# The last block's delta rule: first inverses between z's weight steps, solve two items earlier, new load order, z's Silu from a tanh

## Chip, cores, metric

One core of one Trainium2 chip. The metric is the device time of one execution of the whole program in microseconds (us); the kernel before has a median of 2697.6 us over three runs.

## The reference, cut to what matters

The program is a small network over 512 tokens of width 1024 (batch 1): two layers with attention and 16 experts, and then one last block, to which the change belongs. All is fp32.

```python
def second_block(x, ...):
    h = rmsnorm(x, ln1)
    qkv_a, z_a, b_a, a_a, q_b, k_b, v_b = split(h @ w_in)
    y_a = gated_deltanet(qkv_a, z_a, b_a, a_a, ...)      # 4 heads of 128
    y_b = dilated_attention(heads(q_b), heads(k_b), heads(v_b), slopes)   # 8 heads of 64
    x = x + concat([y_a, y_b]) @ w_out
    h = rmsnorm(x, ln2)
    x = x + (silu(causal_dwconv(h @ w_gate)) * (h @ w_up)) @ w_down
    return rmsnorm(x, ln_f)
# in gated_deltanet, by chunks: a = strict(k_beta k^T * decay); (1 + a) sol = [v*beta, k_beta*exp(g)];
# then a scan over the chunks: v_new = u - w S; o = q_dec S + a_qk v_new; S = S*dl + k_dec^T v_new
# y_a = o * rsqrt(mean(o*o)) * norm_gain * silu(z)
```

The kernel takes chunks of 128 tokens, so there are four (t = 0 to 3), and four heads (h).

## The kernel before, in words

The engines run five hand-written programs. Each walks the same list of pieces and does its own part of each, in the order of the list; semaphores tie them together, and every engine takes its work strictly in its own order. For the stretch of this change the list is `second_plan()` (L492 to L549), and `between()` in each engine's program walks it.

**Weights.** Weights come as loads of up to 1 MB into slots (`weight_steps()`, L97). Slots 0 to 2 are the ring RING; slot 3 is the tail of X (X[:, 4:6]). SP issues them in order and waits until the slot is free. For a product in two parts (high and low, fp32r), ACT copies a step of 1024 columns to WHL as its high part (L1474), and DVE (L2015) or POOL (L2793), by turns, subtracts to get the low part. PE then makes three matmuls where one would do. The copies run two steps ahead of PE; they do not cross into the output weights' steps before the piece `early`. WHL shares its memory with the attention's buffers (EB2, ET2, SB2, YH, YBT: "WIDE" in the profile), so the first three steps of the output weights also wait for the last low part of the attention's output ("behind", `V["y2", 7]`). The output weights are `loads[third]` on. Before, the turn through the slots went on from the input weights, so the first of them falls on slot 3, whose memory is the delta rule's scratch WS; SP waits there for the end of the solve (`P["du", 6, 3]`, L793).

**Part one of the list (k = 0 to 15).** PE makes q and k of the attention (`col`), then vb and z (`tok`, four steps each, four token tiles per step; z's four tiles end in the last step). Beside them the delta rule is prepared: norms of q and k (`square`, `sum`, `unit`), turned keys and values, scalars, `decay` h (matmul gb; DVE's differences L2609, ACT's exponentials into WS[h] (the decay) and CMS[h]), and products on POOL (`values`, `keys`, `kdec`). The piece `zsilu` stands at the end: ACT has copied z out of PE's banks (L1838) and then puts Silu over it in place (L1871), which takes a table load before and one behind.

**Part two (items k = 0 to 36).** `attend` k is a pipeline over the 32 pairs of attention head and query tile: score matmul (PE L1255), bias, maximum and sign (DVE L2559 to L2564), exponential (ACT L1809, one item later), transposes (L848) and their copy (L1817), values (PE L1269), scaling (DVE L2575); a pair of heads is turned at the end of its last item (`ybT`, copy L1823). Between the parts of the attention stand those of the delta rule:

- `head` h (k = 0 to 3): PE makes kk (L1326), bb (L1323) and kq (L1326 again). DVE (L2618 to L2630): AT = kk * WS, AT = bb * AT, U0 = mask of AT, then identity minus it, a copy DL, AQ = kq * WS behind POOL's causal mask of WS[h] (L2909), and q times its decay.
- `first` h: transposes of U0 and ACT's copy (L1875). `mask` n, h: POOL's product of AT with the mask of level n (L2917).
- the solve by doubling, levels n = 1 to 6, four heads each: `cm` (PE L1342, ACT's copy L1881), then `onward` (PE L1349 du and L1354 dt, DVE L2635 and L2639).
- `nw` h (L1362, L1885), then the scan: `vnew` t (PE L1374, L1376; ACT L1891), `out` t (PE L1386 ds, L1392/L1393 o; ACT's square L1897; DVE's state L2652/L2655, sum L2659, mean L2661), `gate` t (ACT's root L1902; DVE L2667 to L2676, the last of them with z), `flip` t (transposes L848, copy L1906).

Behind the items comes the tail: `y2` j (high and low parts of the mixed output, L1915 and L2680), `early` (the copies of the output weights' first three steps), and `mix` n, t (output projection of tile t, L1237 to L1239).

**Banks.** PE's eight banks are two rings here: `flow` (0 to 3) for `col`, `tok`, `attend` and `mix`, and `rule` (4 to 7) for the delta rule. Taking a bank waits for the named release of the piece that had it four takes before, for instance `(V, ("kkd", h))`: DVE's first product of head h.

What fixes the place of the pieces before:

```python
for k in range(37):
    if k < 36: plan.append(("attend", k))
    if k < 4: plan.append(("head", k))
    if 1 <= k <= 4: plan += [("first", k - 1), ("mask", 1, k - 1)]
    if 0 <= k - 5 < 24: plan.append(("onward", *wy[k - 5]))
```

## Time and profile before

| | |
|---|---|
| runs | 2700.8, 2697.6, 2692.08 us (median 2697.6) |
| the profiled execution | 2695.96 us, its span 2693.8 us |
| granted clock of TensorE over the span | 0.972 of 2.4 GHz |
| PE busy | 93% of the span |
| DVE, ACT, POOL busy | 48%, 37%, 15% |
| the stretch of `second_plan`'s items to the last turned tile | about 2078 to 2268 us |

The times are those of the slowest (here the only) core. Busy shares are means over stages that differ; the stretches below show the stage in question. The granted clock is 1.00 at 2.4 GHz and 0.50 at 1.2 GHz; a value between is a mean over both. A bracket behind a row says how long the engine had been idle before it, and which instruction ended that.

### The profile page before, as it was taken

What the parts mean: (1) busy time and instruction counts of PE and PEld (TensorE: products, weight loads), DVE (VectorE), ACT (ScalarE), POOL (GpSimd) and SP (SyncE); (2) the same over time, 40 slices, a digit from 0 to 9 for tenths busy, and PEclk for the clock granted to TensorE, in tenths of its full rate; (3) what the DMA queues carried; (4) which work ended last, traced back from release to release, by engine and by line L of the source; (5) the groups of instructions that cost most, each with busy time, mean ns of one, the idle gap of its engine ahead of it and who ended that gap; (6) DMA issues with size and microseconds to landing.
All of it is one profiled execution on the core that took longest, in us unless ns stands there. A gap on an engine that the chain in (4) does not pass through costs nothing.

```text
span 2693.8 us, 35458 instructions
## 1 busy us (share of the span) xinstructions
PE 2513.7 (93%) x13952; PEld 1531.4 (57%) x13952; DVE 1294.7 (48%) x2483; ACT 991.1 (37%) x1862; POOL 408.5 (15%) x276
## 2 busy tenths in 40 slices
PE   6998997899999997997969999998999898999998
PEld 4875565433333332775744344442767787788886
DVE  3596435344444444586352333334664655442342
ACT  5216542334444443526433222223344333322222
POOL 0222102001111101223100000001114311122221
PEclk8999999899999999998989999999999899999999
DMA  6216744699999996320139999998120002222221
GB/s 262 81 47 233 272 153 185 248 335 377 386 386 389 389 389 239 117 78 1 49 147 422 421 421 421 421 421 328 56 86 20 13 22 105 86 94 94 94 87 55
DMA packets 85467, 567.71 MB, mean 211 GB/s; under 512 B 11760, under 2 KB 12016, under 8 KB 20280
## 3 DMA queue, kind: packets, MB, share of 16 engines
q1 hardware_dynamic: 79944, 550.15, 52.0%
q0 software_dynamic: 3616, 11.80, 2.0%
q10 hardware_dynamic: 1744, 3.51, 0.4%
q8 instruction: 112, 1.84, 0.3%
q14 instruction: 51, 0.42, 0.0%
HBM read 550.74 MB, written 14.68 MB: 210 GB/s over the span
## 4 chain that ended last, share of the span: by engine, by line
PE 47%; DVE 3%; DMA 1%; ACT 1%; issue 1%; DVEq 0%; ACTq 0%
PE PS L1108 12%; PE PS L1225 4%; PE PS L1223 4%; PE PS L1224 4%; PE PS L1237 3%; PE PS L1239 3%; PE PS L1238 3%; PE PS L1182 2%; PE PS L1213 2%; PE PS L848 1%; DMA RF<-in_w_down_dram 1%; PE PS L1349 1%; PE PS L1354 1%; PE PS L1269 1%; PE PS L1255 1%
## 5 line engine op out<-in xcount | busy, mean ns | idle before, releaser
L2793 POOL TENSOR_TENSOR WHL<-RING,WHL 128x1024 fp32r<-128x1024 f32 x64 | 172.8, 2700 | 1324.9 <-ACT WHL L1474 1324.9
L1474 ACT ACTIVATE WHL<-RING 128x1024 fp32r<-128x1024 f32 x129 | 134.6, 1047 | 200.4 <-PE PS L1239 129.3
L1223 PE MATMUL PS<-RR,WHL 128*128 128x512 f32 x512 | 205.0, 400 | 2.0 <-DVE RR L2546 1.1
L1225 PE MATMUL PS<-RR,WHL 128*128 128x512 f32 x512 | 203.2, 397 | 0.0
L1224 PE MATMUL PS<-RR,WHL 128*128 128x512 f32 x512 | 201.5, 394 | 0.0
L1108 PE MATMUL PS<-RING,RF 128*64 128x512 f32 x816 | 184.9, 596 | 0.7 <-issue 0.7
L1108 PE MATMUL PS<-WIDE,RF 128*64 128x512 f32 x792 | 183.0, 599 | 0.0
L2015 DVE TENSOR_TENSOR WHL<-RING,WHL 128x1024 fp32r<-128x1024 f32 x65 | 81.8, 1260 | 165.7 <-ACT WHL L1474 159.5
L1760 ACT ACTIVATE RF<-PS,MODS,MSC 128x128 f32<-128x128 f32 x192 | 73.2, 445 | 182.8 <-PE PS L1182 130.5
L1108 PE MATMUL PS<-RF 128*64 128x512 f32 x544 | 127.5, 596 | 0.5 <-DMA RF<-in_w_down_dram 0.5
L1108 PE MATMUL PS<-X,RF 128*64 128x512 f32 x528 | 123.0, 597 | 0.6 <-DMA X<-in_w_down_dram 0.6
L1108 PEld LDWEIGHTS PS<-RING,RF 128*64 128x64 f32 x816 | 55.8, 137 | 111.7 <-issue 104.9
L1108 PEld LDWEIGHTS PS<-WIDE,RF 128*64 128x64 f32 x792 | 54.1, 137 | 113.7 <-issue 109.2
L1239 PE MATMUL PS<-WHL,AS 128*128 128x512 f32 x288 | 114.2, 397 | 0.0
L2475 DVE TENSOR_TENSOR RF<-PS,RF 64x512 f32<-64x512 f32 x64 | 43.5, 680 | 142.0 <-ACT RF L1741 142.0
L2099 DVE SCALAR_TENSOR_TENSOR AR<-AR,VEC 128x497 f32<-128x497 f32 (+29 forms) x180 | 111.7, 697 | 0.0
L1223 PEld LDWEIGHTS PS<-RR,WHL 128*128 128x128 f32 x512 | 96.1, 188 | 27.1 <-issue 4.2
L1224 PEld LDWEIGHTS PS<-RR,WHL 128*128 128x128 f32 x512 | 96.1, 188 | 25.3 <-issue 1.7
L1225 PEld LDWEIGHTS PS<-RR,WHL 128*128 128x128 f32 x512 | 96.1, 188 | 23.2
L2448 DVE TENSOR_TENSOR RF<-PS,RF 64x512 f32<-64x512 f32 x64 | 43.6, 681 | 117.9 <-ACT RF L1706 115.5
L1237 PE MATMUL PS<-WHL,AS 128*128 128x512 f32 x248 | 98.5, 397 | 0.8 <-DVE RF L2310 0.8
L1238 PE MATMUL PS<-WHL,AS 128*128 128x512 f32 x248 | 98.3, 396 | 0.0
(404 smaller groups left out, 5151.0 us busy)
## 6 DMA issues: line engine op xcount, KB each, us to landing
RING<-in_w_gate_dram SPq DMA_DIRECT2D x60, 1024.0 KB, 16.0
WIDE<-in_w_down_dram SPq DMA_DIRECT2D x52, 1024.0 KB, 11.6
RING<-in_ada_w_dram SPq DMA_DIRECT2D x48, 1024.0 KB, 6.1
RING<-in_w_up_dram SPq DMA_DIRECT2D x44, 1024.0 KB, 7.5
X<-in_w_gate_dram SPq DMA_DIRECT2D x39, 1024.0 KB
AR<-in_w_up_dram SPq DMA_DIRECT2D x37, 1024.0 KB, 9.8
RF<-in_w_down_dram SPq DMA_DIRECT2D x31, 1024.0 KB, 13.7
RING<-in_w_in_dram SPq DMA_DIRECT2D x30, 1024.0 KB, 5.1
```

The source lines that it names most:

```text
L1108: ins = e.matmul(a[r:r + 64, :], xs[:, j, 0:64], w[:, i, :], start=begin and i < 2, stop=end and i > 1)
L1223: e.matmul(o, h[:, j, :], HTH2[:, j, :], start=j == 0, stop=False)
L1224: e.matmul(o, h[:, j, :], HTL2[:, j, :], start=False, stop=False)
L1225: ins = e.matmul(o, lo[:, j, :], HTH2[:, j, :], start=False, stop=j == 7)
L1237: e.matmul(o, hi(j)[:, z], h[:, i, :], start=j == 0, stop=False)
L1238: e.matmul(o, hi(j)[:, z], lo[:, i, :], start=False, stop=False)
L1239: ins = e.matmul(o, lo_(j)[:, z], h[:, i, :], start=False, stop=j == k - 1)
L1474: e.activation(h, load_buffer(ld)[:, js, cs], ACT.Copy).then_inc(act, A(("hi", st["i"])))
L1760: e.activation(xs[:, :, a0:a0 + w_], o[:, b0:b0 + 2 * w_].rearrange("p (e s) -> p e s", e=2), ACT.Identity, bias=MODS2[:, l, 24 + jj, s:s ...
L2015: e.tensor_tensor(lo, load_buffer(loads[st["load"]])[:, js, cs], h.bitcast(F32), ALU.subtract).then_inc(dve, V(("lo", st["i"])))
L2099: e.scalar_tensor_tensor(y, UB[:, i, t0 + lo + d:t0 + hi + d], VEC[:, w:w + 1], y, ALU.mult, ALU.add).then_inc(dve, V(*([("conv", l, s)] i ...
L2793: e.tensor_tensor(lo, load_buffer(loads[st["load"]])[:, js, cs], h.bitcast(F32), ALU.subtract).then_inc(pool, G(("lo", st["i"])))
```

## The change

In the list: `causal` h (POOL's mask of the decay) becomes a piece of its own behind `decay`; the old `head` is split in three. `last` h is the copy DL. `head` h keeps kk, bb and U0 and goes to k = 13, 14, 15 and behind them (heads 0 to 3), so two of them stand between z's steps and two behind the last. `query` h is kq, AQ and q's decay and stays at items 0 to 3, with `first` h and `mask` 1, h now in the same item. `cm`, `onward`, `nw` and the scan's first pieces go two items earlier; `vnew` 3 and all before it lie in the items now, and `gate` 2 leads the tail.

z: ACT takes tanh(z/2) out of the bank in place of the copy; DVE makes (tanh + 1) * z, with z read from the bank, at `zsilu`; the bank is free after that. The missing 0.5 goes into the last product of `gate`.

Loads: the turn through the slots starts anew at the output weights, so they take slots 0, 1, 2 and then 3.

```diff
--- before.py
+++ after.py
@@ -181,7 +181,8 @@
     for ld in loads:
-        turn, slots = (0 if ld["slots"] != slots and slots[:3] != ld["slots"][:3] else turn + 1), ld["slots"]
+        new = ld["slots"] != slots and slots[:3] != ld["slots"][:3]
+        turn, slots = (0 if new or ld is loads[third] else turn + 1), ld["slots"]
         k = slots[turn % len(slots)]
@@ -513,38 +514,39 @@
             plan += [("decay", k - 10), ("keys", k - 10)]
+        if 11 <= k <= 14:
+            plan.append(("causal", k - 11))
+        if k == 13:
+            plan += [("last", h) for h in range(4)] + [("head", 0)]
         if k == 14:
...
         if k >= 14:
-            plan += [("kdec", 2 * (k - 14)), ("kdec", 2 * (k - 14) + 1)]
-    plan.append(("zsilu",))
+            plan += [("kdec", 2 * (k - 14)), ("kdec", 2 * (k - 14) + 1), ("head", k - 13)]
+    plan += [("head", 3), ("zsilu",)]
 
...
               ("out", 2), ("flip", 1), ("vnew", 3), ("gate", 2), ("out", 3), ("flip", 2), ("gate", 3), ("flip", 3)]
-    starts = {("vnew", 0): 30, ("out", 0): 31, ("vnew", 1): 32, ("gate", 0): 32, ("out", 1): 33, ("flip", 0): 34}
+    starts = {("vnew", 0): 28, ("out", 0): 29, ("vnew", 1): 30, ("gate", 0): 30, ("out", 1): 31, ("flip", 0): 32,
+              ("vnew", 2): 33, ("gate", 1): 34, ("out", 2): 35, ("flip", 1): 36, ("vnew", 3): 36}
     for k in range(37):
...
         if k < 4:
-            plan.append(("head", k))
-        if 1 <= k <= 4:
-            plan += [("first", k - 1), ("mask", 1, k - 1)]
-        if 0 <= k - 5 < 24:
-            plan.append(("onward", *wy[k - 5]))
-        if 0 <= k - 4 < 24:
-            n, h = wy[k - 4]
+            plan += [("query", k), ("first", k), ("mask", 1, k)]
+        if 0 <= k - 3 < 24:
+            plan.append(("onward", *wy[k - 3]))
+        if 0 <= k - 2 < 24:
+            n, h = wy[k - 2]
             plan.append(("cm", n, h))
...
                 plan.append(("mask", n + 1, h))
-        if 26 <= k < 30:
-            plan.append(("nw", k - 26))
-        while chunks and k >= starts.get(chunks[0], 35 if chunks[0][0] != "flip" else 36):
+        if 24 <= k < 28:
+            plan.append(("nw", k - 24))
+        while chunks and k >= starts.get(chunks[0], 37):
             plan.append(chunks.pop(0))
-            if chunks and chunks[0] not in starts:
-                break
-    assert chunks[0] == ("out", 2)
-    plan += [("out", 2), ("flip", 1), ("y2", 4), ("y2", 5), ("y2", 6), ("y2", 7), ("vnew", 3), ("gate", 2), ("early",),
+    assert chunks[0] == ("gate", 2)
+    plan += [("gate", 2), ("y2", 4), ("y2", 5), ("y2", 6), ("y2", 7), ("early",),
              ("out", 3), ("flip", 2), ("mix", 0, 0), ("gate", 3), ("mix", 0, 1), ("mix", 0, 2), ("flip", 3), ("mix", 0, 3)]
@@ -1290,7 +1292,7 @@
                     elif what == "tok":
-                        tokens(flow, (k[0],), A, 8, k[1], lambda j: HTH2[:, j, :], lambda j: HTL2[:, j, :])
+                        tokens(flow, (k[0],), V if k[0] == "z" else A, 8, k[1], lambda j: HTH2[:, j, :], lambda j: HTL2[:, j, :])
                     elif what == "attend":
@@ -1317,14 +1319,18 @@
                         h, = k
-                        for name, f, free in (("kk", 4 + h, "kkd"), ("bb", 0, "at"), ("kq", h, "aq")):
-                            o = bank(rule, (name, h), (V, (free, h)))
-                            if name == "bb":
-                                ins = e.matmul(o, HSEL[:, 128 * h:128 * h + 128], BR, start=True, stop=True)
-                            else:
-                                for z in tiles4:
-                                    ins = e.matmul(o[:, z], C[:, 4 + h, z], C[:, f, z], start=True, stop=True)
-                            ins.then_inc(pe, P((name, h)))
+                        o = bank(rule, ("kk", h), (V, ("kkd", h)))
+                        for z in tiles4:
+                            ins = e.matmul(o[:, z], C[:, 4 + h, z], C[:, 4 + h, z], start=True, stop=True)
+                        ins.then_inc(pe, P(("kk", h)))
+                        o = bank(rule, ("bb", h), (V, ("at", h)))
+                        e.matmul(o, HSEL[:, 128 * h:128 * h + 128], BR, start=True, stop=True).then_inc(pe, P(("bb", h)))
+                    elif what == "query":
+                        h, = k
+                        o = bank(rule, ("kq", h), (V, ("aq", h)))
+                        for z in tiles4:
+                            ins = e.matmul(o[:, z], C[:, 4 + h, z], C[:, h, z], start=True, stop=True)
+                        ins.then_inc(pe, P(("kq", h)))
                     elif what == "first":
@@ -1832,11 +1838,12 @@
                         weights()
-                        if n == 6:
-                            for t in range(4):
-                                e.wait_ge(pe, P[name, t])
-                                e.activation((VB if name == "vb" else Z)[:, t, :], held(name, t), ACT.Copy
-                                             ).then_inc(act, A((name, t)))
+                        for t in range(4 if n == 6 else 0):
+                            e.wait_ge(pe, P[name, t])
+                            if name == "vb":
+                                e.activation(VB[:, t, :], held(name, t), ACT.Copy).then_inc(act, A((name, t)))
+                            else:
+                                e.activation(Z[:, t, :], held(name, t), ACT.Tanh, scale=0.5).then_inc(act, A(("ztanh", t)))
                     elif what == "attend":
@@ -1865,10 +1872,6 @@
                         e.activation(KDC, KDC, ACT.Exp).then_inc(act, A(("kdc",)))
-                    elif what == "zsilu":
-                        e.wait_ge(act, A["z", 3])
-                        for t in range(4):
-                            e.activation(Z[:, t, :], Z[:, t, :], ACT.Silu).then_inc(act, A(("zsilu", t)))
                     elif what == "first":
@@ -2583,6 +2586,11 @@
                         attend2(*k)
+                    elif what == "zsilu":
+                        for t in range(4):
+                            e.wait_ge(act, A["ztanh", t])
+                            e.scalar_tensor_tensor(Z[:, t, :], Z[:, t, :], 1.0, held("z", t), ALU.add, ALU.mult
+                                                   ).then_inc(dve, V(("z", t)))
                     elif what == "sum":
@@ -2614,7 +2622,7 @@
                         e.wait_ge(pe, P["kk", h])
-                        e.wait_ge(act, A["egb", h])
+                        e.wait_ge(pool, G["causal", h])
                         e.tensor_tensor(AT[:, h, :], held("kk", h), WS[h], ALU.mult).then_inc(dve, V(("kkd", h)))
@@ -2623,9 +2631,13 @@
                         e.scalar_tensor_tensor(u3, u3, -1.0, idb, ALU.mult, ALU.add).then_inc(dve, V(("u0", h)))
+                    elif what == "last":
+                        h, = k
+                        e.wait_ge(act, A["egb", h])
                         e.tensor_copy(DL[:, h, :], CMS[h].rearrange("p (t i) -> p t i", i=128)[:, :, 127]).then_inc(dve, V())
+                    elif what == "query":
+                        h, = k
                         e.wait_ge(pe, P["kq", h])
-                        e.wait_ge(pool, G["causal", h])
                         e.tensor_tensor(AQ[:, h, :], held("kq", h), WS[h], ALU.mult).then_inc(dve, V(("aq", h)))
@@ -2671,9 +2683,9 @@
                                         ).then_inc(dve, V())
-                        e.wait_ge(act, A["zsilu", t])
+                        e.wait_ge(dve, V["z", t])
                         e.wait_ge(dve, V.n)
-                        e.tensor_tensor(os_, os_, Z[:, t, :], ALU.mult).then_inc(dve, V(("gated", t)))
+                        e.scalar_tensor_tensor(os_, os_, 0.5, Z[:, t, :], ALU.mult, ALU.mult).then_inc(dve, V(("gated", t)))
                     elif what == "y2":
@@ -2902,10 +2914,10 @@
                     e.tensor_tensor(KTOK[:, t, :, :], KTOK[:, t, :, :], by_token(KDC, t), ALU.mult).then_inc(pool, G(("kdec", t)))
-                elif what == "head":
+                elif what == "causal":
                     h, = k
                     d3 = WS[h].rearrange("p (t i) -> p t i", i=128)
-                    e.wait_ge(dve, V["kkd", h])
+                    e.wait_ge(act, A["dec", h])
                     e.tensor_tensor(d3, d3, cau, ALU.mult).then_inc(pool, G(("causal", h)))
...
```

## Rows read from the trace of the kernel before

**Rows 1.** The profile's page, busy time, share of the span and instructions of each engine.

```profile
PE 2513.7 (93%) x13952; PEld 1531.4 (57%) x13952; DVE 1294.7 (48%) x2483; ACT 991.1 (37%) x1862; POOL 408.5 (15%) x276
```

**Rows 2.** Busy us by 4 us stretch: PE, PEld, DVE, ACT, POOL, then PEclk, DMA share, GB/s.

```profile
2094.00:2098.00 4.00, 0.37 (x2) 0.37 (x2) 3.93 (x7) 0.00 (x0) 1.29 (x1) 0.80 0.00 0
2098.00:2102.00 4.00, 4.00 (x12) 2.33 (x11) 1.36 (x5) 0.98 (x3) 1.06 (x1) 0.50 0.00 0
2106.00:2110.00 4.00, 3.36 (x17) 3.36 (x17) 2.48 (x9) 1.79 (x4) 1.27 (x1) 0.50 0.22 70
2232.00:2236.00 4.00, 3.84 (x21) 3.84 (x22) 1.30 (x5) 1.19 (x3) 0.00 (x0) 0.61 0.03 10
2260.00:2264.00 4.00, 3.60 (x12) 3.06 (x13) 3.90 (x3) 0.60 (x1) 2.47 (x1) 0.57 0.00 0
```

**Rows 3.** PE's timeline, head: start us, us, engine line op, out<-in, xcount [idle before <-releaser].

```profile
2082.54 1.16 PE L1326 MATMUL PS<-AR 128*128 128x128 f32 x8
2083.63 1.12 PE L1323 MATMUL PS<-VECY,ROUTER 4*128 4x512 f32 x2
2084.68 1.16 PE L1326 MATMUL PS<-AR 128*128 128x128 f32 x8
...
2097.63 0.69 PE L1269 MATMUL PS<-AR,WIDE 128*128 128x64 f32 x2 [4.52 <-DVE WIDE L2559]
...
2106.64 0.90 PE L848 MATMUL PS<-CON,WIDE 128*128 128x128 f32 x3 [0.93 <-DVE WIDE L2559]
...
2110.45 0.70 PE L1255 MATMUL PS<-RF 64*128 64x256 f32 x2
...
2112.19 1.11 PE L1349 MATMUL PS<-RF,X 128*128 128x128 f32 x8
```

**Rows 4.** DVE's timeline, head.

```profile
2079.88 0.69 DVE L2618 TENSOR_TENSOR RF<-PS,X 128x512 f32<-128x512 f32 x1 [11.55 <-PE PS L1326]
...
2094.20 1.63 DVE L2625 SCALAR_TENSOR_TENSOR RF<-RF,CON 128x512 f32<-128x512 f32 x1
```

**Rows 5.** ACT's timeline, z's copies and the table load behind them.

```profile
2074.16 0.60 ACT L1838 ACTIVATE AR<-PS 128x512 f32<-128x512 f32 x1 [4.58 <-PE PS L1239]
...
2078.38 0.60 ACT L1838 ACTIVATE AR<-PS 128x512 f32<-128x512 f32 x1 [0.80 <-PE PS L1239]
2078.99 1.28 ACT L1871 ACT_TABLE_LOAD   x1
```

**Rows 6.** PE's timeline, tail.

```profile
2217.66 0.49 PE L1255 MATMUL PS<-RF 64*128 64x128 f32 x2
...
2218.85 1.11 PE L1349 MATMUL PS<-RF,X 128*128 128x128 f32 x8
...
2232.16 0.66 PE L1269 MATMUL PS<-AR,WIDE 128*128 128x64 f32 x4 [1.89 <-DVE WIDE L2559]
...
2243.77 1.09 PE L848 MATMUL PS<-CON,WIDE 128*128 128x128 f32 x4 [2.25 <-DVE WIDE L2575]
...
2260.40 1.09 PE L848 MATMUL PS<-CON,RF 128*128 128x128 f32 x4 [2.87 <-DVE RF L2676]
...
2267.39 0.63 PE L848 MATMUL PS<-CON 128*128 128x128 f32 x4 [0.66 <-DVE CON L2676]
```

**Rows 7.** ACT's, DVE's and POOL's timelines, tail.

```profile
2236.78 1.28 ACT L1902 ACT_TABLE_LOAD   x1
2238.08 0.20 ACT L1902 ACTIVATE SM<-SM 128x4 f32<-128x4 f32 x1
...
2240.05 0.69 DVE L2676 TENSOR_TENSOR RF<-RF,AR 128x512 f32<-128x512 f32 x1
...
2253.46 2.49 DVE L2680 TENSOR_TENSOR RR<-WIDE,RR 128x512 fp32r<-128x512 f32 x4
...
2257.25 2.45 POOL L2793 TENSOR_TENSOR WHL<-X,WHL 128x1024 fp32r<-128x1024 f32 x1 [56.11 <-ACT WHL L1474]
```

**Rows 8.** SP's timeline, the output weights' first load.

```profile
2219.99 0.33 SPq L815 DMA_DIRECT2D X<-in_w_out_dram  x1
```

## The prediction

> **What bounds the kernel now.** The page comes first: PE is busy 93% of the 2693.8 us [rows 1], so a change can only win where PE waits or runs at half clock. The changed code runs from about 2045 to 2270 us, between the expert layers and the last feed-forward. The table of 4 us stretches shows the two places there where PE loses time. From 2094 to 2098 PE is busy 0.37 of 4 us, and in the stretch behind it the granted clock is 0.50, which is the 1.2 GHz level instead of 2.4. From 2232 and from 2260 it is 0.61 and 0.57 [rows 2]. In the solve that lies between the two places PE hardly waits.
>
> PE's timeline names the waits. In the head (attention items 0 to 4, with the four preparations of the inverse) PE waits 4.52 us and 0.93 us for DVE L2559, the score's bias, which stands in DVE's queue behind the long "head" entries. The 8 matmuls of a key product take 1.16 us before the long wait; from it to 2110 the clock stays at 0.50, and all of PE's work takes about double [rows 2, 3]. The first solve step, onward(1,0), starts at 2112.19. DVE shows why it is late: a head entry is six or seven products of 0.69 us one behind another, and one that meets POOL takes 1.63 [rows 4].
>
> In the tail (2230 to 2267) the waits are many and short: 1.89, 2.25 and 2.87 us are the largest, until the last turned tile at 2267.39; from there on PE works through [rows 6]. The solve in between, 24 steps of about 4.7 us, is PE's own work and the change leaves it alone.
>
> **The change part by part, against the profiled execution (2695.96 us; 1.6 under the median of the three runs, 2697.6).**
>
> Load order: three of the output weights' four loads leave earlier, in front of the solve's end. Before, the first is issued at 2219.99 [rows 8], but the copies of these weights start only when the attention's four low parts are written, at 2253.46 + 2.49 = 2255.95; POOL's share begins at 2257.25 [rows 7]. The loads land in between. SP has nothing else to issue that is needed, and the next gate load waits for these same copies either way. Zero. If the cover were gone it would be one load's landing, a few us.
>
> z's Silu: four ACT products and two table loads (1.28 each, [rows 5]) leave ACT, which is not the bound there; four tanh take the place of the four copies at the same price. If tanh wants a load of its own, it fits in ACT's idle 4.58 us before z's first copy [rows 5]. Zero on ACT. On DVE four products of 0.69 us are added (about 2.5 us overlapped), and they now free z's banks. The first score of the attention takes z's first bank, so it waits for DVE.
>
> Head. PE's parts of a head cost 1.09 (kk) and 1.05 (bb), from start to start [rows 3]. Two of each now go between z's steps: z ends 4.3 us later than 2078.2, at 2082.5 (its four tiles come 1.41 apart, [rows 5]). The other two follow: 2086.8. DVE has done heads 0 and 1 under z's matmuls. Head 2 can start at 2083.5; two heads of four chained products, each 0.69 [rows 4] and some 0.04 of hand-over, are 5.9, so 2089.4. Then comes z's first product, 2090.1. **Here is the wait that takes the old one's place: PE 3.4 us, behind z's bank.** Then PE has four query products (4.3), four groups of transposes (0.5 each: 1.09 at half clock in [rows 6]), the first cm (1.0, eight matmuls like bb) and the attention parts of items 0 to 3 (3.5, an estimate: one later item is 1.19 to 1.74 [rows 3, 6], these lack most of it). That is 10.8, so onward(1,0) at 2100.9. DVE's query entries are two products each instead of seven and keep up. Before, it began at 2112.19, but with items 4 and 5 behind it, 1.19 + 1.74 = 2.9. Gain 11.3 - 2.9 = 8.4 at full clock.
>
> Clock in the head: a wait of 3.4 us stands between the 1.89 and 2.87 of the tail (the next 4 us had 0.61 and 0.57, so were low for some 3 us, [rows 2, 6]) and the 4.52 (low for 12.5 us, [rows 2, 3]). Half of that is lost: 1.5 to 6.2. I take 2: two of the three rows of such waits have the short form. Head: 6.4 gained, bounds 2.2 and 8.4.
>
> Solve: two items earlier against the attention, same work. 0.
>
> Tail. I count from item 28's first score (2217.66 before, [rows 6]). Before, 49.7 us from there to the last turned tile. Two nw products and the last onward (eight matmuls each, 2.8 in all) now lie ahead of item 28, so an unchanged tail would be 46.9. The new order puts gate 0 in item 30, before the last two exponentials instead of behind them. ACT's table goes to Sqrt, back to Exp and to Sqrt again: two loads more. The new chain, with t from item 28: PE is full until vnew 1 ends, 9.5. Copy 0.7, load and root 1.5, gate 0 on DVE 2.5 (in the trace 2.66 from the root's start to the product's end, [rows 7]): 14.2. Only then DVE reaches item 30's bias, maximum and sign, 1.3, then the exponential 0.8: 16.3. PE had finished at 13.8: 2.5 us idle. Output 1's square and sum stand before item 31's bias (as output 0's did in the old order: PE's 1.89 at item 32 is that, [rows 6]): bias from 18.1, so PE waits another 2.1, and exp 31 ends at 20.5. Transposes, values and vnew 2 (16 matmuls, twice a head part, 1.8) to 23.5; copy, load, root to 25.7; first product of gate 1 to 26.7, whose bank output 2 wants; output 2 to 28.6; state to 29.8; vnew 3 to 31.6; copy and root to 32.5; gate 2 to 35.0; four low parts 2.5 [rows 7] to 37.5; the weight's copy 1.0 and POOL's low part 2.45 [rows 7] and their hand-overs, 41.3: the output projection starts. Three quarters of its step, 4.2, and the last turned tile at 46.7. Gate 2 no longer runs into POOL, which gives back what the middle lost. So at full clock the tail gains 0.2. Clock: the two waits of 2.5 and 2.1 lie together with 0.5 us of work between, so the clock falls there; the old tail's losses are in its 49.7. I take 2.5 more (bounds 0 and 6).
>
> Sum: 6.4 + 0.2 - 2.5 = **4 us gained**: 2692.0 for the profiled execution, 2693.6 against the median.
>
> The Trainium skill speaks against one step. The row: the table load at 2236.78 takes 1.28 us and the root starts 0.02 behind it [rows 7], so a switch costs 1.3 here. "ScalarE: Activation LUTs", What ACT_TABLE_LOAD costs, gives about 2.66 us for every switch, a drain of 1.38 included. By that the two switches on the tail's chain (gates 0 and 1) would be 2.8 us dearer and the gain 1.2; the row shows no such drain, and the trace decides.
>
> **The rivals.**
>
> A, the gain in full. The clock stays high, or the tail's waits overlap better than my chain has them. For: the solve's middle holds full clock through its short waits. Against: each of the four longer waits here was followed by half clock. 8.6 and up to 14, with the old tail's clock losses gone as well: 2687 (2689 to 2683.6).
>
> B, the wait only moves. DVE's block in gate 0 of item 30 eats the head's gain whole, because the tail is bound by the chain DVE to ACT to PE, not by work: starting it earlier with more in it buys nothing. The loss needed is 4 more than my count. For: eight hand-overs in my chain, each 0.1 to 0.3 too short. 2697.6 (2695 to 2700).
>
> C, slower by the clock. PE's half clock behind the 3.4 us wait lasts 12.5 us, as after 4.52 [rows 2, 3], cost 6.2; and the tail, which from t = 14 on has wait behind wait, stays at 1.2 GHz to the end. Its PE work on the chain (values, vnew 2, output 2, vnew 3, three quarters of the projection's step, about 12) doubles. 8.6 - 6.2 - 12 = 10 lost: 2707. It decides once clock losses pass 8.6. Against: the old tail came back to 1.00 each time.
>
> D, dearer switches. If each load made ACT idle as long again, 1.3, twice on the chain: 2.6 of the 4 us, 2696.2. (The Trainium skill's "ScalarE: Activation LUTs", What ACT_TABLE_LOAD costs, has such a drain; the row at 2238.08 does not.)
>
> **How the numbers follow.** Forecast 0.47 (2690 to 2696), A 0.23, B 0.18, C 0.07, D 0.05. About 0.3%, 8.1 us, is what a measurement of this kernel can tell from no change. Faster by more: most of A, 0.22. Slower by more: most of C and little else, 0.07. Same: 0.71. The likeliest is 2693.6. The range reaches through A to 12.6 gained and past B's upper end: 2685 to 2701. Left out are C (0.07), the far part of A (0.05) and as much of the unnamed on either side.
>
> **What would show it.** Head: kk and bb of heads 0 and 1 between z's steps, PE's one wait of about 3.4 us behind DVE's product on z's bank, at about 2087; onward(1,0) within 2 us of 2103 (2101 if the clock holds). No Silu load; three table loads in the tail instead of one, each 1.28. PE's waits for DVE's bias line around item 32, 2 to 5 us in all; a wait of 5 to 6 us before the projection's first matmul, and the last turned tile at about 2263.5. The forecast is wrong if the clock row behind z stays at 1.00, if onward(1,0) starts after 2106, or if the tail from item 28 is shorter than 45 us or longer than 52.

## The result, and the profile after

The change makes the kernel a little slower: 2703.8 us (median of 8 runs, 2699.89 to 2707.32) against 2694.26 us (8 runs of the kernel before, 2692.08 to 2700.8). The medians lie 9.5 us apart; the ratio is 1.0027, with a 95% interval of 1.0019 to 1.0036, which is 5 to 10 us, about 7. 4 us less than before had been forecast. The sign is clear. Whether the loss passes the 0.3% up to which the prediction called it no change is not: the interval reaches over it.

The prediction counted from 2697.6 us, the median of the first three runs of the kernel before; with eight it is 2694.26. So its likeliest time, 2693.6, was missed by 10.2 us, but the change itself by 11 (4 gained forecast, 7 lost).

Against [rows 1] the page says nothing of where the time went; PE is still busy 93%, in a longer span:

```profile
span 2699.6 us, 35454 instructions
...
PE 2516.1 (93%) x13952; PEld 1532.9 (57%) x13952; DVE 1294.6 (48%) x2487; ACT 988.7 (37%) x1858; POOL 410.3 (15%) x276
```

Runs differ by some us before the changed code begins. So every profile below is measured by one ruler that leaves this out: **the stretch** from the start of PE's product gb of head 3 (the last `decay`, between z's second and third step) to the start of the last turned tile of the tail, the row of 2267.39 in [rows 6]. What follows the stretch takes 426.4 to 426.5 us to the end of the span in every kernel of this study. The stretch took 201.6 us before and 208.6 after: 7.0 us more, which fits the measured ratio. Its parts:

| from the stretch's start to | before | forecast | after |
|---|---|---|---|
| onward(1,0), the first solve step | 46.4 | 37.1 | 38.7 |
| item 28's first score | 151.9 | 148.4 | 150.4 |
| the output projection's first matmul | 195.4 | 192.2 | 202.0 |
| the last turned tile | 201.6 | 197.6 | 208.6 |
| item 28 to the last turned tile | 49.7 | 49.2 | 58.3 |

(The forecast's numbers are the prediction's, counted from 2065.78, where the stretch began in the profile before.)

PE's timeline after, in the head. The columns are start, duration, engine and line, operation, tiles, shape, count, and the wait before it with what ended it. PE has both products of heads 2 and 3, then waits for DVE's product on z's first bank:

```profile
2081.21 1.06 PE L1324 MATMUL PS<-AR 128*128 128x128 f32 x8
2082.19 1.12 PE L1327 MATMUL PS<-VECY,ROUTER 4*128 4x512 f32 x2
2083.24 1.16 PE L1324 MATMUL PS<-AR 128*128 128x128 f32 x8
2084.33 1.12 PE L1327 MATMUL PS<-VECY,ROUTER 4*128 4x512 f32 x2
2089.00 0.79 PE L1257 MATMUL PS<-RF 64*128 64x128 f32 x2 [3.54 <-DVE AR L2592]
2089.72 2.07 PE L1332 MATMUL PS<-AR 128*128 128x128 f32 x8
...
2103.25 1.06 PE L1355 MATMUL PS<-RF,X 128*128 128x128 f32 x8
```

That is the wait the prediction named, 3.54 us for 3.4. The 4.52 of [rows 3] is gone. Behind the new one a query product takes 2.07 us instead of 1.16, and in the table of 4 us stretches (busy us of PE, PEld, DVE, ACT and POOL, then the granted clock) the clock stands at 1.2 GHz for two stretches and most of a third is back:

```profile
2084.00:2088.00 4.00, 1.45 (x6) 0.50 (x4) 3.83 (x7) 0.00 (x0) 0.00 (x0) 0.91 0.01 2
2088.00:2092.00 4.00, 3.00 (x12) 2.78 (x13) 2.91 (x6) 0.00 (x0) 0.00 (x0) 0.50 0.00 0
2092.00:2096.00 4.00, 4.00 (x16) 3.02 (x15) 1.93 (x6) 1.09 (x3) 1.27 (x1) 0.50 0.00 0
2096.00:2100.00 4.00, 4.00 (x25) 2.86 (x24) 2.96 (x8) 1.78 (x5) 1.27 (x1) 0.81 0.00 0
```

PE's timeline in the tail, all of its waits but two of under 0.5 us:

```profile
2222.84 0.33 PE L850 MATMUL PS<-CON,WIDE 128*128 128x128 f32 x1 [1.11 <-DVE WIDE L2562]
...
2227.42 1.12 PE L1257 MATMUL PS<-RF 64*128 64x512 f32 x2
2232.62 0.69 PE L850 MATMUL PS<-CON,WIDE 128*128 128x128 f32 x2 [4.08 <-DVE WIDE L2562]
...
2241.19 1.11 PE L1271 MATMUL PS<-AR,WIDE 128*128 128x64 f32 x4 [2.59 <-DVE WIDE L2562]
...
2254.96 0.46 PE L1380 MATMUL PS<-AR,RF 128*128 128x128 f32 x2 [0.97 <-DVE RF L2664]
...
2257.76 0.46 PE L1398 MATMUL PS<-RF,AR 128*128 128x128 f32 x2 [0.78 <-ACT SM L1905]
...
2260.33 0.63 PE L850 MATMUL PS<-CON,RF 128*128 128x128 f32 x4 [0.54 <-DVE RF L2688]
2266.58 0.80 PE L1239 MATMUL PS<-WHL,RR 128*128 128x512 f32 x1 [5.62 <-POOL WHL L2805]
```

The three waits for DVE L2562 are waits for a bank of `flow`. L850's row of 2 is the transposes of item 29: they take the bank that item 30's scores held four takes earlier, and DVE frees it only with item 30's bias. Before the projection PE waits 5.62 us; 5 to 6 had been forecast. PE's waits of the tail add up to 16.5 us with the two small ones, against 10.2 before (the bracketed waits of [rows 6] and 0.73, 0.97 and 0.78 between them). The tail grew by 8.5 us while 2.8 us of work had moved out of it, so 11.3 are to be explained: 6.3 are waits, and the other 5.0 fit work at half clock. What the low clock cost can be worked out by itself: PE's busy time in each us of the trace, times what the granted clock lacks to 1.00, adds up to 4.7 us before and 10.0 after, 5.3 more.

ACT and DVE show what DVE did in the time of the 4.08:

```profile
2228.14 1.28 ACT L1905 ACT_TABLE_LOAD   x1
2229.43 0.20 ACT L1905 ACTIVATE SM<-SM 128x4 f32<-128x4 f32 x1
2229.65 1.28 ACT L1815 ACT_TABLE_LOAD   x1
2233.38 0.61 ACT L1815 ACTIVATE WIDE<-WIDE,SM 128x384 f32<-128x384 f32 x1 [2.44 <-DVE SM L2567]
```

```profile
2224.09 0.28 DVE L2578 TENSOR_SCALAR WIDE<-PS,SM 128x64 f32<-128x64 f32 x1 [0.59 <-PE PS L1271]
2229.67 0.18 DVE L2679 RECIPROCAL SM<-SM 128x4 f32<-128x4 f32 x1 [5.30 <-ACT SM L1905]
...
2231.40 0.69 DVE L2688 SCALAR_TENSOR_TENSOR RF<-RF,AR 128x512 f32<-128x512 f32 x1
2232.01 0.55 DVE L2562 TENSOR_TENSOR WIDE<-PS,AR 128x384 f32<-128x384 f32 x1
```

DVE stands idle 5.30 us for gate 0's root, with item 30's bias behind it in its queue; PE's transposes start 0.06 us after the bias is done. For 3.2 of the 5.30 us ACT is itself idle: the copy of vnew 1 stands ahead of the root in its queue, and PE ends vnew 1 only at 2227.5. Copy, table load and root are the rest.

### The profile page after: what moved, and what is told of

Same layout as the page of the kernel before. It is cut to its first block, busy times and chain, and to the rows that moved or that the text cites. A ratio compares the mean times of both kernels' runs of the same rounds, so it can differ in the third digit from the quotient of the medians.

```text
span 2699.6 us, 35454 instructions
## 1 busy us (share of the span) xinstructions
PE 2516.1 (93%) x13952; PEld 1532.9 (57%) x13952; DVE 1294.6 (48%) x2487; ACT 988.7 (37%) x1858; POOL 410.3 (15%) x276
## 4 chain that ended last, share of the span: by engine, by line
PE 47%; DVE 3%; ACT 1%; DMA 1%; issue 1%; POOL 0%; DVEq 0%; ACTq 0%
PE PS L1110 12%; PE PS L1225 4%; PE PS L1226 4%; PE PS L1227 4%; PE PS L1239 3%; PE PS L1240 3%; PE PS L1241 3%; PE PS L1184 2%; PE PS L1215 2%; PE PS L850 1%; DMA RF<-in_w_down_dram 1%; PE PS L1355 1%; PE PS L1257 1%; PE PS L1360 1%; PE PS L1271 1%
## 5 line engine op out<-in xcount | busy, mean ns | idle before, releaser
L1225 PE MATMUL PS<-RR,WHL 128*128 128x512 f32 x512 | 205.4, 401 | 2.7 <-DVE RR L2549 1.8
L1227 PE MATMUL PS<-RR,WHL 128*128 128x512 f32 x512 | 202.0, 394 | 0.0
L2102 DVE SCALAR_TENSOR_TENSOR AR<-AR,VEC 128x497 f32<-128x497 f32 (+29 forms) x180 | 111.7, 696 | 0.0
## 6 DMA issues: line engine op xcount, KB each, us to landing
WIDE<-in_w_down_dram SPq DMA_DIRECT2D x52, 1024.0 KB, 11.4
RF<-in_w_down_dram SPq DMA_DIRECT2D x31, 1024.0 KB, 13.8
```

Of the source, the lines that this page charges most:

```text
L1225: e.matmul(o, h[:, j, :], HTH2[:, j, :], start=j == 0, stop=False)
L1227: ins = e.matmul(o, lo[:, j, :], HTH2[:, j, :], start=False, stop=j == 7)
L2102: e.scalar_tensor_tensor(y, UB[:, i, t0 + lo + d:t0 + hi + d], VEC[:, w:w + 1], y, ALU.mult, ALU.add).then_inc(dve, V(*([("conv", l, s)] i ...
```

## The experiments

All are built from the changed kernel unless it is said. The ratio is to the kernel before, timed on the same chip.

**1. The scan and the tail back at their old items.** The new head, solve, loads and z stay.

```diff
-    starts = {("vnew", 0): 28, ("out", 0): 29, ("vnew", 1): 30, ("gate", 0): 30, ("out", 1): 31, ("flip", 0): 32,
-              ("vnew", 2): 33, ("gate", 1): 34, ("out", 2): 35, ("flip", 1): 36, ("vnew", 3): 36}
+    starts = {("vnew", 0): 30, ("out", 0): 31, ("vnew", 1): 32, ("gate", 0): 32, ("out", 1): 33, ("flip", 0): 34}
...
-        while chunks and k >= starts.get(chunks[0], 37):
+        while chunks and k >= starts.get(chunks[0], 35 if chunks[0][0] != "flip" else 36):
...
-    plan += [("gate", 2), ("y2", 4), ("y2", 5), ("y2", 6), ("y2", 7), ("early",),
+    plan += [("out", 2), ("flip", 1), ("y2", 4), ("y2", 5), ("y2", 6), ("y2", 7), ("vnew", 3), ("gate", 2), ("early",),
```

> The changed kernel with the scan (vnew, out, gate, flip) and the tail's order put back at the items of the kernel before; head, solve, load order and z stay changed. The stretch from the start of decay's last product (gb of head 3) to the last turned tile took 201.6 us before and 208.6 us after; item 28 begins 151.9 and 150.4 us into it. Theory: 9 us were lost behind item 28, by the scan's new place and the tail's new order. Then the part behind item 28 is about 47 to 49 us instead of 58.3, the stretch 197 to 199 us and the time 2691 to 2693. Rival: the loss comes from the other parts (z's product on DVE, the loads, a lower clock behind the head's wait): the stretch stays at 206 us or more and the time at 2700 or more.

Measured: stretch 197.2 us, item 28 at 150.6, the part behind it 46.7; 2692.8 us, ratio 0.9996 (0.9984 to 1.0009). The theory holds. All of the loss, 11.4 us of the stretch, lies in the scan's and the tail's new order; without it no difference to the kernel before can be measured. PE's wait at item 30 is gone, and those from item 32 on are the old ones again; PE's timeline:

```profile
2227.18 0.66 PE L1272 MATMUL PS<-AR,WIDE 128*128 128x64 f32 x4 [1.88 <-DVE WIDE L2563]
...
2237.31 1.09 PE L851 MATMUL PS<-CON,WIDE 128*128 128x128 f32 x4 [2.25 <-DVE WIDE L2579]
...
2254.21 0.96 PE L851 MATMUL PS<-CON,RF 128*128 128x128 f32 x4 [2.87 <-DVE RF L2689]
...
2261.22 0.63 PE L851 MATMUL PS<-CON 128*128 128x128 f32 x4 [0.61 <-DVE CON L2689]
```

**2. The attention's high and low parts ahead of vnew 3 and gate 2.** Only this.

```diff
-              ("vnew", 2): 33, ("gate", 1): 34, ("out", 2): 35, ("flip", 1): 36, ("vnew", 3): 36}
+              ("vnew", 2): 33, ("gate", 1): 34, ("out", 2): 35, ("flip", 1): 36}
...
-    plan += [("gate", 2), ("y2", 4), ("y2", 5), ("y2", 6), ("y2", 7), ("early",),
+    plan += [("y2", 4), ("y2", 5), ("y2", 6), ("y2", 7), ("vnew", 3), ("gate", 2), ("early",),
```

> The changed kernel with one thing different: the high and low parts of the attention's output (y2 4 to 7) stand ahead of vnew 3 and gate 2 again, as before. Theory: after, these parts wait for gate 2 (low parts from 2260.1, though the last attention tile was turned by 2251), and the output projection behind them. With them first the projection starts 3 to 4 us earlier and the stretch from decay's last product to the last turned tile is 204 to 206 us instead of 208.6. Rival: the chain of gate 3 to the last turned tile is what ends last; the projection starts earlier and then waits for it, and the stretch stays between 207.5 and 209.

Measured: stretch 205.4 us, the projection's first matmul at 198.8 instead of 202.0; 2700.0 us, ratio 1.0014 (1.0005 to 1.0024). The theory holds: 3.2 us. Most of the wait does move, as the rival had it (the turned tile of output 2 waits 3.05 us instead of 0.54, and the last one 2.19 us for gate 3's product, where it had not waited over 0.5), but the sum is a gain: PE waits 0.9 us less, and the projection runs at full clock from its start, where 2.5 us had been lost behind the wait of 5.62.

**3. z's products ahead of heads 2 and 3.**

```diff
-            plan += [("kdec", 2 * (k - 14)), ("kdec", 2 * (k - 14) + 1), ("head", k - 13)]
-    plan += [("head", 3), ("zsilu",)]
+            plan += [("kdec", 2 * (k - 14)), ("kdec", 2 * (k - 14) + 1)]
+        if k == 15:
+            plan.append(("zsilu",))
+        if k >= 14:
+            plan.append(("head", k - 13))
+    plan.append(("head", 3))
```

> The changed kernel with z's four products on DVE ahead of heads 2 and 3 instead of behind them. Theory: the 3.54 us wait of PE for z's bank in front of item 0's scores goes, since DVE has nothing to do before kk of head 2, and the half clock behind it (2089 to 2098) goes with it: item 28 begins 143 to 146 us into the stretch instead of 150.4, the whole stretch 201 to 204 us. Rival: DVE is late for heads 2 and 3 then, and PE waits for the banks of kq and of the first transposes instead; item 28 begins at 149 us or later.

Measured: stretch 201.9 us, item 28 at 143.4, 7.0 us earlier; 2697.1 us, ratio 1.0009 (0.9999 to 1.0018). The theory holds. PE goes from bb of head 3 into item 0's scores without a wait, and the queries behind run at full clock:

```profile
2085.95 1.12 PE L1331 MATMUL PS<-VECY,ROUTER 4*128 4x512 f32 x2
2087.00 0.49 PE L1261 MATMUL PS<-RF 64*128 64x128 f32 x2
2087.42 1.16 PE L1336 MATMUL PS<-AR 128*128 128x128 f32 x8
```

Of the 7.0 us the wait is 3.5, and a new one of 0.54 at item 2 takes some of it back; the other 4.0 are the half clock that the wait set off. The tail is 58.5 us, as bad as before the repair: an earlier head does nothing for it.

**4. The two parts costed at nothing, in the kernel before.** The new load order and z's tanh and product, no piece moved.

```diff
+        turn, slots = (0 if new or ld is loads[third] else turn + 1), ld["slots"]
...
-                        e.wait_ge(act, A["z", 3])
-                        for t in range(4):
-                            e.activation(Z[:, t, :], Z[:, t, :], ACT.Silu).then_inc(act, A(("zsilu", t)))
+                        for t in range(4):
+                            e.wait_ge(act, A["ztanh", t])
+                            e.scalar_tensor_tensor(Z[:, t, :], Z[:, t, :], 1.0, held("z", t), ALU.add, ALU.mult
...
```

> The kernel before with the two parts that the prediction costed at nothing: the new load order and z's tanh and product; no piece of the list is moved. Theory: nothing to see but z's products on DVE in front of item 0 (2.5 us, part of it hidden); the stretch is 201.6 to 204 us, the time within 3 us of the kernel before. Rival: one of them costs by itself, for instance the three early loads beside the attention's bias or the scores waiting for z's bank with half clock behind: 205 us or more.

Measured: 2696.1 us, ratio 1.0005 (0.9992 to 1.0017): no difference. The stretch, 197.8 us, lies below the theory's 201.6 to 204. 1.6 of the 3.8 stand in the head, behind the same 4.52 us wait, where the clock comes back earlier; the rest is in the tail, where the first half of vnew 1 ran at full clock in this profile and the wait of 2.25 us was 1.59. As the time did not follow, this is not claimed as a gain. Together the two parts cost nothing that can be measured, by the interval at most 5 us.

**5. Gate 0 behind the last exponential.** From item 30 to item 32, behind output 1; flip 0 to item 33.

```diff
-    chunks = [("vnew", 0), ("out", 0), ("vnew", 1), ("gate", 0), ("out", 1), ("flip", 0), ("vnew", 2), ("gate", 1),
+    chunks = [("vnew", 0), ("out", 0), ("vnew", 1), ("out", 1), ("gate", 0), ("flip", 0), ("vnew", 2), ("gate", 1),
...
-    starts = {("vnew", 0): 28, ("out", 0): 29, ("vnew", 1): 30, ("gate", 0): 30, ("out", 1): 31, ("flip", 0): 32,
+    starts = {("vnew", 0): 28, ("out", 0): 29, ("vnew", 1): 30, ("out", 1): 31, ("gate", 0): 32, ("flip", 0): 33,
```

> The changed kernel with one piece moved: gate 0 stands in item 32 behind output 1 instead of in item 30 ahead of it, flip 0 in item 33. The part behind item 28 took 58.3 us after, 49.7 before and 46.7 with the scan and tail at their old places; the order of the y2 parts alone gave 3.2 of that. Theory: gate 0 between the last two exponentials is the rest. DVE then makes item 30's and 31's bias in time, PE's wait of 4.08 us at item 32 and most of the 2.59 behind it go, and two of three table loads. The stretch from decay's last product to the last turned tile is 202 to 205 us instead of 208.6. Rival: the rest lies in the scan's place as such (more pieces per item, the sums of output 0 and 1 ahead of the biases, vnew 1 at half clock): the stretch stays at 206.5 us or more.

Measured: stretch 205.1 us, 2699.9 us, ratio 1.0015 (1.0002 to 1.0028). The part behind item 28 fell from 58.3 to 52.9 us. The head, which this kernel shares with the changed one, was 1.8 us slower in this profile (the first solve step at 40.5 instead of 38.7), and that is why the stretch as a whole misses the theory's 205 by 0.1. Two of the tail's three table loads are gone with the move, and PE's wait of 4.08 us, but the 2.59 stays, which the theory had going too, and a wait of 2.10 for gate 0's product is new:

```profile
2236.22 1.12 PE L1271 MATMUL PS<-AR,WIDE 128*128 128x64 f32 x4 [2.59 <-DVE WIDE L2562]
2238.07 1.09 PE L850 MATMUL PS<-CON,WIDE 128*128 128x128 f32 x4 [0.73 <-ACT WIDE L1815]
...
2242.43 1.09 PE L850 MATMUL PS<-CON,RF 128*128 128x128 f32 x4 [2.10 <-DVE SM L2571]
```

So 5.3 us are gate 0's place with the two table loads that it brings, 3.2 the parts of y2. PE's waits in the tail are only 1.8 us fewer; the other 3.5 are time no longer lost to the low clock. Some 3 us of the tail's 11.6 (58.3 less 46.7) are left, by single repairs; with both repairs together 4.1 are (experiment 8).

**6. No table switch.** The roots of gate become copies; what is left out is the square root in the delta rule's norm.

```diff
-                        e.activation(r4, r4, ACT.Sqrt).then_inc(act, A(("orms", t)))
+                        e.activation(r4, r4, ACT.Copy).then_inc(act, A(("orms", t)))
```

> The changed kernel with the four roots of gate (ACT, 128x4) replaced by a plain copy of the same size, so that ACT's table is not switched in the tail; what is left out is the square root in the delta rule's norm. Two of the three loads (gates 0 and 1) lie on the chain. Theory: a switch costs its 1.28 us and no more; the stretch shortens by 2.0 to 3.5 us, to 205 to 206.6. Rival (the Trainium skill's ScalarE: Activation LUTs, What ACT_TABLE_LOAD costs, about 2.66 us for every switch): 5 us or more, to 203.6 or less. Second rival: the loads are beside the chain, and the stretch stays within 1 us of 208.6.

Measured: stretch 205.2 us, 3.5 less; 2701.2 us, ratio 1.0013 (1.0 to 1.0027). PE's wait shrinks from 4.08 to 2.66 us, by 1.4, about one load. All of its waits in the tail are 1.3 us fewer, and the low clock costs 2.3 less; so the 3.5 lie near the 2.6 of two loads, but no more than that is shown. In ACT's rows of the changed kernel the load starts 0.02 us behind the copy and the root 0.01 behind the load, so a load costs its 1.28 us and no more.

By the 2.66 us per switch of the Trainium skill ("ScalarE: Activation LUTs", What ACT_TABLE_LOAD costs) an estimate of two switches is 5.3 us here; the rows do not show it. The Trainium skill's "ScalarE: Activation LUTs", Table sets: the hidden batching unit, advises to finish all the exponentials before the roots. Experiment 5 bears that out, though more through DVE's queue than through the loads: without any load PE still waits 2.66 of the 4.08 us.

**7. Both repairs together** (experiments 1 and 3).

> The changed kernel with both repairs: z's products on DVE ahead of heads 2 and 3, and the scan and tail back at the places of the kernel before. Theory: the two are independent. Item 28 begins at 143.4 us as with the first alone, the part behind it takes 46.7 us as with the second alone; the stretch is 190 us against 201.6 before, the time 11 us under the kernel before, ratio 0.9957. Rival: an earlier head gives the tail no less to wait for; the tail grows by the 3 to 7 us and the ratio is 0.998 or more.

Measured: stretch 190.2 us, item 28 at 143.4, the part behind it 46.9; 2685.8 us, ratio 0.9961 (0.9947 to 0.9974). Faster than both kernels, 9.4 us under the kernel before of the same chip (2695.2), and the two repairs add up: 11.4 and 6.7 us of stretch alone, 18.4 together. A wait of 1.02 us at item 29 comes in: PE wants the bank of item 28's scores there, and DVE, 0.97 us idle, gets this head's bias from the DMA only then.

**8. The scan left two items earlier, its faults mended** (experiments 2, 3 and 5).

> The changed kernel with the scan left two items earlier, but its three faults mended: z's products ahead of heads 2 and 3, gate 0 in item 32 behind output 1, and the attention's y2 parts ahead of vnew 3. Theory: the scan two items earlier is worth nothing by itself, because the tail is a chain of hand-overs; the part behind item 28 is 48 to 52 us and the stretch 191 to 195 us, no better than with the old places. Rival: once the faults are gone the earlier scan gains its two items, and the stretch is 188 us or less.

Measured: stretch 194.3 us, the part behind item 28 50.9; 2689.2 us, ratio 0.9977 (0.9966 to 0.9989). The theory holds: the scan two items earlier is worth nothing, and costs 4.1 us against its old place. (The times, 2689.2 and 2685.8, were taken on the same chip and lie 3.5 us apart; their intervals overlap.)

**9. The sums out of the bias's way**, on top of 8.

```diff
                     elif what == "out":
...
-                        e.wait_ge(act, A["osq", t])
-                        e.wait_ge(dve, V.n)
-                        e.tensor_reduce(r4, os_.rearrange("p (h d) -> p h d", d=128), AX.X, ALU.add).then_inc(dve, V())
-                        e.wait_ge(dve, V.n)
-                        e.tensor_scalar(r4, r4, 1.0 / 128, EPS, ALU.mult, ALU.add).then_inc(dve, V(("oms", t)))
                     elif what == "gate":
...
+                        e.wait_ge(act, A["osq", t])
+                        e.wait_ge(dve, V.n)
+                        e.tensor_reduce(r4, os_.rearrange("p (h d) -> p h d", d=128), AX.X, ALU.add).then_inc(dve, V())
+                        e.wait_ge(dve, V.n)
+                        e.tensor_scalar(r4, r4, 1.0 / 128, EPS, ALU.mult, ALU.add).then_inc(dve, V(("oms", t)))
```

> The kernel with the scan two items earlier and its three faults mended, and on top DVE's sum and mean of output t taken out of the piece out and put at the start of gate t, so that no attention bias stands behind ACT's square. The part behind item 28 took 50.9 us without this and 46.9 with the scan at its old places. Theory: the 1.11 and 2.59 us waits of PE for DVE's bias line (items 30 and 32) come from these sums; they shrink by 2 us or more, the clock holds longer, and the part is 47.5 to 49.5 us, the whole stretch 191 to 193. Rival: the state of output 1, which waits for PE's output itself, holds the bias back just as long; the stretch stays within 1 us of 194.3.

Measured: stretch 192.4 us, the part behind item 28 49.1; 2688.3 us, ratio 0.9976 (0.9965 to 0.9986). The wait of 1.11 us at item 30 is gone and that of 2.59 is 1.60, as the theory had it. But later waits grew, and all of PE's waits in the tail are 13.1 us for 12.4; what fell is the cost of the low clock, from 6.7 to 3.8 us. The stretch is 1.9 us shorter, the time the same within the noise (ratio 0.9977 before the shift), so a gain is not shown here. The rest of item 32's wait is output 1's state, which DVE makes only when PE has read the old one.

**10. The same shift on top of 7.**

> The kernel with z's products ahead of heads 2 and 3 and the scan and tail at their old places (stretch 190.2 us), and the same shift of the sums into gate. Theory: gate t needs the sum at once, so the sum moves onto the chain in front of gate 1 and gate 2 while only item 32 gains its bias 1 us earlier; the stretch is 189.5 to 192.5 us, no gain that can be measured against 190.2. Rival: the 1.89 us wait at item 32 and the half clock behind it go, and the stretch is 188 us or less.

Measured: stretch 186.9 us, the part behind item 28 43.5; 2682.6 us, ratio 0.9952 (0.9939 to 0.9966), the best of all. The stretch is the rival's and below the theory's 189.5 to 192.5. The theory had the sum on the chain in front of gates 1 and 2. But item 32's wait fell from 1.89 to 0.35, the clock did not fall behind it, and the turned attention tile waits 1.26 us instead of 2.26:

```profile
2222.11 0.66 PE L1276 MATMUL PS<-AR,WIDE 128*128 128x64 f32 x4 [0.35 <-DVE WIDE L2567]
...
2231.25 0.63 PE L855 MATMUL PS<-CON,WIDE 128*128 128x128 f32 x4 [1.26 <-DVE WIDE L2583]
```

```profile
2221.74 1.06 PE L1276 MATMUL PS<-AR,WIDE 128*128 128x64 f32 x4 [1.89 <-DVE WIDE L2567]
...
2233.50 0.63 PE L855 MATMUL PS<-CON,WIDE 128*128 128x128 f32 x4 [2.26 <-DVE WIDE L2583]
```

(The first fence is this kernel, the second experiment 7's.) What it costs is seen later: the tile of output 2 waits 3.73 us instead of 2.87. PE's waits are 1.7 us fewer than in experiment 7, and the low clock costs 1.8 less. The second part may be luck of the profile: in experiment 1, with the tail in the same order, the clock stayed at 1.00 behind item 32's wait of 1.88 us too. Experiments 7 and 10 were not timed against each other on one chip, and their intervals against the kernel before overlap; it is the stretch, 190.2 against 186.9 us, that tells them apart.

**11. The changed kernel once more**, one profile.

> The changed kernel unchanged, a second profile, to see how far one kernel's stretch differs from profile to profile. If the stretch from decay's last product to the last turned tile is 206.5 to 210.5 us again (208.6 in the first), the differences of 3 us and more between the kernels are theirs; if it differs by more than 2 us, only the larger ones are.

Measured: 208.8 us for 208.6, item 28 at 150.5. The run took 2706.2 us, 4.4 more than the first profiled one, and the stretch began 4.3 us later than there, so the difference between these two runs lies in what comes before.

The tails of all kernels side by side, from item 28's first score to the last turned tile, in us. The third number is worked out as in the section above. What the two leave of the tail is 31.8 to 32.6 us everywhere but before, where 2.8 us more work stands in it.

| kernel | tail | PE's waits | lost to the low clock |
|---|---|---|---|
| before | 49.7 | 10.2 | 4.7 |
| after | 58.3 | 16.5 | 10.0 |
| 1, scan and tail old | 46.7 | 10.9 | 3.2 |
| 2, y2 first | 55.0 | 15.6 | 7.5 |
| 5, gate 0 later | 52.9 | 14.6 | 6.5 |
| 6, no table switch | 54.7 | 15.2 | 7.7 |
| 7, both repairs | 46.9 | 11.1 | 3.4 |
| 8, scan early, mended | 50.9 | 12.4 | 6.7 |
| 9, and the sums later | 49.1 | 13.1 | 3.8 |
| 10, 7 and the sums later | 43.5 | 9.4 | 1.6 |

Not tried: a root without ACT (as a power on DVE), gate 0's root ahead of vnew 1's copy in ACT's queue, more banks for the attention, and the load order by itself.

## Why the prediction was wrong, point by point

**What bounds the kernel, and the head: right in mechanism.** PE loses time in the two places named. The new order of the head, the wait behind z's bank (3.4 forecast, 3.54 measured) and its releaser are as foretold. The first solve step came at 38.7 us of the stretch; 37.1 had been forecast, of which 2 were for the clock. The term mis-sized is "I take 2": the clock stayed low from about 2088 to 2098, and experiment 3 prices it at 4.0 us. It was inside the bounds given, 1.5 to 6.2; the work in front of the first solve step was some 0.4 us less than counted.

**Load order, z's Silu: costed at zero, and nothing that can be measured** (experiment 4). Tanh took no table load: none stands between z's products and gate 0 in ACT's timeline.

**Solve: right.** From the first solve step to item 28 it is 111.7 us after; 105.5 before and the 5.8 of work that moved in make 111.3.

**Tail: wrong, by 9.1 us** (49.2 forecast, 58.3 measured). The step that failed is the sentence "PE had finished at 13.8: 2.5 us idle". The chain had DVE's and ACT's queues right, and even gate 0's block, but let PE run through item 31 beside it. PE could not: in item 31 the transposes of item 29 take the bank of item 30's scores, which the bias behind gate 0 frees. Output 1 stood behind these transposes, and so started at 18.5 us behind item 28's score (2233.42) instead of at 11.0 (the chain's 9.5 and item 31's attention parts); its sum, item 31's bias and exponential all came later by that. 4.08 of the 7.5 us are this wait. The other 3 had come before it: vnew 1 ended at 12.5 instead of 9.5, by the 1.11 us wait that the chain did not have, which is the same rule one item earlier with output 0's sum in front of item 29's bias, and by the low clock behind it. In the old order gate 0 came after the last exponential and had no bias behind it; of this kind there was only the 1.89 at item 32, which the prediction had read rightly. Gate 0's place is 5.3 us (experiment 5).

The second fault was costed as a credit. "Gate 2 no longer runs into POOL" is true: its last product takes 0.69 us now. But the chain itself had the low parts end at 37.5 instead of ahead of gate 2, and left it at that; the old order, in which gate 2's last product takes 2.83 us beside POOL, is 3.2 us faster (experiment 2). Doing a piece first takes its wait off that piece and puts it on whatever the queue holds behind, here on the part that the projection waited for longest.

The third is the clock: "2.5 more" was 5.0 to 5.3, inside the bounds of 0 and 6. There were more and longer waits ahead of it.

The chain's last step does not add up: the projection starts at 41.3, three quarters of its step are 4.2, and that makes 45.5 and not 46.7. Measured it was 6.6 us from the projection's first matmul to the last turned tile, more than half of it at 1.2 GHz.

**The rivals.** A is out for the change as it stands; its size, not its account, came with both repairs (2685.8 against 2695.2 us, experiment 7). B named the right piece, gate 0 in item 30, but as the end of the loss, 4 us; it was the largest single part, 5.3, of 11.6. C had the sign and nearly the size (10 us lost against 7 to 9.5) by the wrong account: the clock took 4.0 in the head, not 6.2, and some 5 in the tail, not 12, where it came back to 1.00 from 2248 to 2264; the other 6.3 in the tail are waits. That its time lies close to the measured one is luck. D is out: the root starts 0.01 us behind its load.

**The chances.** Slower by over 0.3% had 0.07, and the measured 0.27% (0.19 to 0.36) lies at its edge; the range, 2685 to 2701, missed the measured time by 3 us, since its upper end rested on B's "eight hand-overs, each 0.1 to 0.3 too short" and took in no wait that the chain lacked.

## What to carry to other kernels

When a piece moves to another place in a list that several in-order engines walk, follow three things for it, not two: the queue it stands in, the piece behind it in that queue, and whose memory bank that piece frees. A ring of four banks with three takes per item makes two engines wait for each other an item apart, and that is not seen in the durations. And pulling work forward pays where it closes a gap and not where the end is a chain of hand-overs: with both repairs the new head had item 28's score 8.5 us earlier (143.4 for 151.9), while the scan two items earlier cost 4.1 us of the stretch even with its faults mended. What pays there is to take a wait away from a queue that others stand in (z's products; for the sums it is not settled), all the more where PE's clock falls behind the wait.

## What the runs showed that was not expected

- A wait of 3.54 us of PE cost another 4.0 us at the 1.2 GHz level (experiment 3), more than itself. A wait of 1.11 us, too, had vnew 1 behind it at 0.59 of the clock (2224 to 2228 after), which took 3.6 us instead of 1.8. But the length of a wait alone does not tell: behind the wait of 2.26 us in experiment 7 the clock stayed at 1.00, and behind item 32's wait of 1.88 us in experiment 1 as well, where behind the same wait before it was 0.61.
- How long the low level lasts differs between profiles of the same code: it ended some 8 us behind the end of the 4.52 us wait in experiment 4 and some 12 us behind it before, and the same head gave 38.7 to 38.9 us to the first solve step in four kernels and 40.5 in a fifth (experiment 5). The tail of the kernel before took 49.7 us, and in experiment 4, with its pieces in the same order, 47.6. Single differences of about 2 us in a stretch with such waits say nothing.
- DVE products with two operands in SBUF stretch when POOL works: gate 2's last product took 0.69 us after, where POOL was idle, and 2.64 in experiment 7, where POOL's low part ran beside it. "SBUF — State Buffer", SBUF: two separate sides, in the Trainium skill, has the two share a pair of ports that one holds for a whole instruction. This case's rows agree: before, POOL's first low part ends at 2259.70 [rows 7], and the product, begun at 2257.59, ends 2.66 us later, 0.55 behind it. DVE's timeline of the changed kernel, that of experiment 7, and POOL's of experiment 7:

```profile
2259.49 0.69 DVE L2688 SCALAR_TENSOR_TENSOR RF<-RF,AR 128x512 f32<-128x512 f32 x1
```

```profile
2246.00 2.64 DVE L2693 SCALAR_TENSOR_TENSOR RF<-RF,AR 128x512 f32<-128x512 f32 x1
```

```profile
2245.65 5.21 POOL L2810 TENSOR_TENSOR WHL<-RING,WHL 128x1024 fp32r<-128x1024 f32 x2 [59.09 <-ACT WHL L1485]
```
